# Expert weights in 4 MB transfers with 32 KB runs, and token rows dealt in fours

## The reference

```python
for e in range(N_EXPERTS):                       # 32
    gu = t @ w_gate_up[e] + b_gate_up[e]         # [1024] -> [2048]
    gate = jnp.minimum(gu[:, :D_EXPERT], SWIGLU_LIMIT)
    up = jnp.clip(gu[:, D_EXPERT:], -SWIGLU_LIMIT, SWIGLU_LIMIT)
    h = (up + 1.0) * (gate * jax.nn.sigmoid(SWIGLU_ALPHA * gate))
    out = out + comb[:, e:e + 1] * (h @ w_down[e] + b_down[e])
```

## Time and profile before

| what | value |
|---|---|
| time, median of 3 runs | 1209.77 us (1209.13 to 1209.91) |
| time of the profiled execution | 1210.05 us |
| its span | 1208.3 us |
| TensorE busy | 1169.4 us, 97% of the span |
| DMA | 446.82 MB, mean 370 GB/s |
| expert weights from 2 MB transfers in the ring | 125 of gate/up, 61 of down |

### The profile page before, as it was taken

How to read it: one execution, slowest core, us unless ns; L and a number is a source line. 1 busy time by engine, 2 the same in 40 slices (tenths; PEclk the granted TensorE clock), 3 DMA queues, 4 the chain that set the end, 5 groups by cost and what they waited for, 6 DMA issues and landing times.

```text
span 1208.3 us, 14638 instructions
## 1 busy us (share of the span) xinstructions
PE 1169.4 (97%) x5836; PEld 553.0 (46%) x5836; DVE 331.4 (27%) x864; ACT 213.7 (18%) x420; POOL 29.2 (2%) x64
## 2 busy tenths in 40 slices
PE   9999999999999999999989899999998999799997
PEld 7777777443443434343333333434434343334344
DVE  4844214250322222131312120313222212111223
ACT  2556302112010101101010112120101010101034
POOL 2001000000000000000000020000000000000000
PEclk9999999999999999999999999999999999999999
DMA  9935573679999999999999999999999999999961
GB/s 287 360 141 203 173 279 133 237 283 429 427 428 426 427 426 428 427 427 429 427 428 428 427 428 425 429 427 426 430 426 428 427 428 430 425 428 428 426 260 40
DMA packets 53287, 446.82 MB, mean 370 GB/s; under 512 B 8174, under 2 KB 11470, under 8 KB 28424
## 3 DMA queue, kind: packets, MB, share of 16 engines
q1 hardware_dynamic: 50512, 440.04, 87.8%
q0 software_dynamic: 2464, 5.71, 1.6%
q10 hardware_dynamic: 256, 0.30, 0.1%
HBM read 444.51 MB, written 1.88 MB: 369 GB/s over the span
## 4 chain that ended last, share of the span: by engine, by line
PE 78%; DMA 20%; ACT 1%; DVE 1%; issue 1%; SPq 0%; DVEq 0%
PE ps L1201 31%; PE ps L864 16%; DMA ring<-in_w_gate_up 14%; PE ps L1222 11%; PE ps L1236 4%; PE ps L1083 3%; DMA ring<-in_w_down 3%; DMA ring<-in_w_ple_gate 2%; PE ps L1016 2%; PE ps L1355 2%; PE ps L1178 2%; PE ps L1168 1%; PE ps L898 1%; PE ps L858 1%; PE ps L885 1%; PE ps L1076 1%
## 5 line engine op out<-in xcount | busy, mean ns | idle before, releaser
L1201 PE MATMUL ps<-ring,work 128*64 128x512 f32 x2000 | 443.6, 597 | 2.8 <-DMA ring<-in_w_gate_up 2.6
L1201 PEld LDWEIGHTS ps<-ring,work 128*64 128x64 f32 x2000 | 141.2, 138 | 273.6 <-issue 261.9
L1222 PE MATMUL ps<-ring,work 128*64 128x512 f32 x992 | 223.4, 595 | 19.4 <-DMA ring<-in_w_down 19.4
L864 PE MATMUL ps<-work,ring 128*128 128x288 f32 x736 | 180.6, 407 | 0.0
L864 PEld LDWEIGHTS ps<-work,ring 128*128 128x128 f32 x736 | 139.7, 190 | 39.6 <-issue 1.7
L1222 PEld LDWEIGHTS ps<-ring,work 128*64 128x64 f32 x992 | 70.6, 137 | 146.8 <-issue 127.6
L2122 DVE TENSOR_SCALAR work<-ps 128x512 f32<-128x512 f32 x32 | 22.1, 691 | 374.5 <-PE ps L1201 374.5
L2094 DVE TENSOR_TENSOR work<-ps,gain_pairs 128x256 f32<-128x256 f32 x60 | 25.5, 424 | 286.2 <-PE ps L1083 286.2
L1626 ACT ACTIVATE work<-work 128x512 f32<-128x512 f32 x32 | 20.2, 631 | 442.9 <-DVE work L2122 442.9
L1083 PE MATMUL ps<-work,x_tok 128*128 128x128 f32 x512 | 65.4, 285 | 0.0
L1083 PEld LDWEIGHTS ps<-work,x_tok 128*128 128x128 f32 x512 | 61.8, 197 | 3.9 <-issue 2.0
(11 more groups left out here) (286 smaller groups left out, 663.0 us busy)
## 6 DMA issues: line engine op xcount, KB each, us to landing
ring<-in_w_gate_up SPq DMA_DIRECT2D x125, 2048.0 KB, 29.5
ring<-in_w_down SPq DMA_DIRECT2D x61, 2048.0 KB, 29.6
ring<-in_w_in SPq DMA_DIRECT2D x7, 2048.0 KB, 19.0
work<-in_w_gate_up SPq DMA_DIRECT2D x3, 1536.0 KB, 12.9
ring<-in_w_proj_b SPq DMA_DIRECT2D x2, 2048.0 KB, 10.0
ring<-in_w_proj_a SPq DMA_DIRECT2D x2, 2048.0 KB, 10.1
ring<-in_w_out SPq DMA_DIRECT2D x2, 2048.0 KB, 9.4
ring<-in_w_ple_gate SPq DMA_DIRECT2D x4, 1024.0 KB, 28.6
```

The costliest lines, as they stand in the source:

```text
L864: mm = pe.matmul(out(b), lhs, rhs, start=(k == 0), stop=(k == len(pairs) - 1))
L1201: mm = pe.matmul(ps[half(g), b, :], xg[:, k, i % 2, :], blocks[2 * (k % 2) + at][:, 512 * g:512 * g + 512], start=False, stop=(k == KC - 1))
L1222: mm = pe.matmul(ps[half(g), b, :], hT_of[i % 2][:, 4 * j + k, :], blocks[k][:, 512 * g:512 * g + 512], start=False, stop=(4 * j + k == KC ...
```

## The change

- From piece 48 on (quad 2) two adjacent pieces come as one transfer of 4 MB, into two neighbouring places of the ring. A partition gets four rows of gate/up, or eight of down, in one run of 32 KB. SP waits before it for the second of the two pieces that held the places. The very last transfer stays apart: one of 2 MB and two of 1 MB.
- TensorE waits for the whole 4 MB before it uses the first of its pieces (`wait_expert_piece` waits on the first place's semaphore).
- The places of the ring are renumbered (`FRONT`, `MOE_SLOT`, `spare`), so that the two of each transfer are neighbours.
- Rows in fours ask for inputs in the same grouping. For pair 2 and later (`in_fours`) the pieces are read with that row order, also where they are still moved in 2 MB. ACT rewrites the two prompt tiles once in pair 1, `deal_inputs`, so that the gather reads contiguous columns, and eight small copies do it for the sample rows. GpSimd loads a second form of the gains, `gain_fours`.
- Down with eight rows in a partition asks that the two halves of the hidden values interleave. So every gate/up matmul, from pair 0 on, reads its moving row in runs of four elements with a step of eight (`dealt`), and its bias row too.

```diff
+        def two_pieces(q):
+            return ring[:, MOE_SLOT[q]:MOE_SLOT[q] + 2, :, :].rearrange("p s a b -> p (s a b)")
+        def dealt(row, g):
+            return row.rearrange("p (c g k) -> p c g k", g=2, k=RUN)[:, :, g, :]
+        def in_fours(m):
+            return not (isinstance(m, int) and m < 2)
...
             s, turn = place(Q, i, q)
-            eng.wait_ge(piece_landed[s], turn * 16 + 16)
+            first, turn = (s, turn) if isinstance(Q, int) and Q < OPENING else \
+                place(Q, *STREAM[STREAM.index((i, q)) // 2 * 2])
+            eng.wait_ge(piece_landed[first], turn * 16 + 16)
...
             def quad_pieces(quads, e0, last=False):
-                for at in range(QUAD_PIECES):
-                    ring_place_used(quads, at)
+                for at in range(0, QUAD_PIECES, 2):
                     i, q = STREAM[at]
-                    expert_piece((at - EXTRAS) % SLOTS, q, e0 + i, last and at == QUAD_PIECES - 1)
+                    r = (at - EXTRAS) % SLOTS
...
+                    ring_place_used(quads, at + 1)
+                    sp.dma_start(two_pieces(r), expert_rows(q, e0 + i)).then_inc(piece_landed[r], 16)
...
                             mm = pe.matmul(ps[half(g), b, :], xg[:, k, i % 2, :],
-                                           blocks[2 * (k % 2) + at][:, 512 * g:512 * g + 512],
+                                           dealt(blocks[2 * (k % 2) + at], g),
                                            start=False, stop=(k == KC - 1))
...
+            def deal_inputs():
+                for b in B_X:
+                    act.wait_ge(filled[b], inputs_gathered(b, 1, False))
+                for t in range(2):
+                    act.wait_ge(x1_copied, t + 1)
+                    nc.scalar.copy(x_tok[:, t, :].rearrange("p (j k c) -> p j k c", k=RUN, c=P),
+                                   x2[t].rearrange("p (j c k) -> p j k c", k=RUN, c=P)).then_inc(x1_dealt, 1)
+                act.wait_ge(comb_ready, 1)
...
                     if embeds and j == 1:
                         embedding_squares()
+                    if begins and j == 1:
+                        deal_inputs()
                     swish(m, 0)
```

More of the change, by code:

```diff
@@ L64 @@
 SLOTS = 8
[L66 to L70, removed]
+FRONT = [("in", 0, 7), ("in", 2, 0), ("in", 4, 3), ("in", 1, 4), ("in", 3, 5), ("in", 5, 6),
+         ("in", 6, 7), ("in", 7, 0), ("b", 0, 3), ("b", 1, 4), ("a", 0, 5), ("a", 1, 6),
+         ("out", 0, 7), ("out", 1, 0)]
+MOE_SLOT = [1, 2, 3, 4, 5, 6, 7, 0]
+RUN = 4
+DEALT_PARTS = 10
 CHUNK = {("gate", 0): (0, 3, 0), ("gate", 1): (0, 3, 1), ("hT", 1): (0, 3, 2),
@@ L266, in hybrid_layer @@
         iota_pass = sb("iota_pass", [P, PASSES])
-        spare = ring[:, 6:8, :, :].rearrange("p s a b -> p (s a b)")
+        spare = ring[:, 1:3, :, :].rearrange("p s a b -> p (s a b)")
         carved = [0]
@@ L673, in quad_pieces, with piece_half @@
+            def piece_half(q):
+                return slice(RUN * D * (q % 2), RUN * D * (q % 2) + RUN * D)
             def quad_pieces(quads, e0, last=False):
-                for at in range(QUAD_PIECES):
-                    ring_place_used(quads, at)
+                for at in range(0, QUAD_PIECES, 2):
                     i, q = STREAM[at]
-                    expert_piece((at - EXTRAS) % SLOTS, q, e0 + i, last and at == QUAD_PIECES - 1)
+                    r = (at - EXTRAS) % SLOTS
+                    if last and at == QUAD_PIECES - 2:
+                        ring_place_used(quads, at)
+                        sp.dma_start(whole_piece(r), expert_rows(q, e0 + i)[:, piece_half(q)]) \
+                            .then_inc(piece_landed[r], 16)
+                        ring_place_used(quads, at + 1)
+                        place_, src = whole_piece((r + 1) % SLOTS), expert_rows(q + 1, e0 + i)[:, piece_half(q + 1)]
+                        sp.dma_start(place_[:, 0:2 * D], src[:, 0:2 * D]).then_inc(last_half_landed, 16)
+                        sp.dma_start(place_[:, 2 * D:4 * D], src[:, 2 * D:4 * D]).then_inc(last_landed, 16)
+                        continue
+                    ring_place_used(quads, at + 1)
+                    sp.dma_start(two_pieces(r), expert_rows(q, e0 + i)).then_inc(piece_landed[r], 16)
@@ L684, in piece_rows @@
                 e = 4 * quads + i
-                if q < GU_PIECES:
+                if q < GU_PIECES and not in_fours(n // (QUAD_PIECES // 2)):
                     return w_gate_up[0, e, 2 * P * q:2 * P * q + 2 * P, :].rearrange("(p k) c -> p (k c)", k=2)
-                rows = 4 * P * (q - GU_PIECES)
-                return w_down[0, e, rows:rows + 4 * P, :].rearrange("(p k) c -> p (k c)", k=4)
+                return expert_rows(q, e)[:, piece_half(q)]
             def extra_rows(n, k, dst):
@@ L718, in opening_piece @@
                     return
-                later, at = divmod(n, QUAD_PIECES)
-                i, q = STREAM[at]
-                expert_piece(ring_turn(n) % SLOTS, q, 4 * later + i)
+                r = ring_turn(n) % SLOTS
+                sp.dma_start(whole_piece(r), piece_rows(n)).then_inc(piece_landed[r], 16)
             wait_filled(sp, ("gate", 3, 3))
@@ L1067, in _, with gather_samples @@
             turn_residual(1, 0)
-            x_blocks = [x_tok[:, t, :].rearrange("p (j c k) -> p j k c", c=P, k=2) for t in range(TT - 1)]
-            def gather_samples():
+            x_pairs = [x_tok[:, t, :].rearrange("p (j c k) -> p j k c", c=P, k=2) for t in range(TT - 1)]
+            x_fours = [x_tok[:, t, :].rearrange("p (j k c) -> p j k c", c=P, k=2) for t in range(TT - 1)]
+            def gather_samples(fours=False):
+                rows = sample_fours if fours else sample_rows
                 for k in range(2):
@@ L1075, in gather_samples, with gather_tile @@
                         own = own_quarter(q)
-                        pe.matmul(ps[:, b, k * P:k * P + P], sample_rows[own, k, :], sel[TT - 1][own, :],
+                        pe.matmul(ps[:, b, k * P:k * P + P], rows[own, k, :], sel[TT - 1][own, :],
                                   start=(k == 0), stop=False)
-            def gather_tile(q, t):
+            def gather_tile(q, t, fours=False):
                 last = t == TILES[-1]
+                x_blocks = x_fours if fours else x_pairs
                 for k in range(2):
@@ L1157, in gather @@
                     pe.wait_ge(emptied[b], inputs_gathered(b, m, late) - 1)
-                gather_samples()
+                if isinstance(m, int) and m == 2:
+                    pe.wait_ge(x1_dealt, DEALT_PARTS)
+                gather_samples(in_fours(m))
                 for q in range(QUARTERS):
                     for t in TILES[1:]:
-                        gather_tile(q, t)
+                        gather_tile(q, t, in_fours(m))
             def turn_hidden(m, s):
@@ L1177, in begin_sums @@
                 for g in range(2):
+                    row = bias_parts[0:BIAS_ROWS, at:at + D]
                     pe.matmul(ps[half(g), b, :], pick[0:BIAS_ROWS, :],
-                              bias_parts[0:BIAS_ROWS, at + 512 * g:at + 512 * g + 512],
+                              row[:, 512 * g:512 * g + 512] if kind == "out" else dealt(row, g),
                               start=True, stop=False)
@@ L1606, in copy_residual @@
                     nc.scalar.copy(x2[t], x1[t]).then_inc(x1_copied, 1)
+            def deal_inputs():
[6 more added lines that the diff above has]
+                act.wait_ge(comb_ready, 1)
+                src = flat_x[:, 2 * D:2 * D + QW].rearrange("p (c g k) -> p g k c", g=2, k=2)
+                for j in range(2):
+                    for g in range(2):
+                        for h in range(2):
+                            nc.scalar.copy(sample_fours[own_quarter(2 * j + g), :, 64 * h:64 * h + 64],
+                                           src[own_quarter(2 * j + h), g, :, :]).then_inc(x1_dealt, 1)
             def embedding_squares():
@@ L2092, in gathered @@
                     own = slice(2 * j, 2 * j + 2)
-                    gains = gain_pairs[:, own].unsqueeze(2).unsqueeze(3).to_broadcast([P, 2, 2, CAP])
+                    gains = (gain_fours if in_fours(m) else gain_pairs)[:, own].unsqueeze(2).unsqueeze(3) \
+                        .to_broadcast([P, 2, 2, CAP])
                     V.tensor_tensor(xg[:, own, :, :], ps[:, b, 0:2 * P].rearrange("p (c i s) -> p c i s", c=2, i=2), gains,
```

30 lines of the change are left out of this document (15 added, 15 removed).

## The result

The changed kernel takes 1224.64 us (median of 4 runs, 1224.0 to 1225.06) against 1209.45 us for the kernel before, a ratio of 1.0126 with a 95% interval of 1.0114 to 1.0138. It is slower by 15 us, 1.3%. The prediction was 1225.4. The profiled execution took 1225.06 us with a span of 1223.3, 15.0 us longer than the span before.

A forecast was written before the change was run, and what follows sets the result against it. Transfers set the pace, TensorE 4 to 5 us a pair faster. Queue standing 18.1 less 5.4 saved lands the last pieces at 1161.1; plus 23.38 gives 1184.5, 15.6 us later: 1225.7, less 0.28, 1225.4 us; range 1206.5 to 1230.

The forecast's parts named there:

- What long runs save: Weight stream, pieces 48 to 189: 71 transfers of 4 MB in 32 KB runs save 76 ns each, 5.4 us in all.
- The coarser step at the end: Pieces 188 and 189: TensorE starts when both have landed; 2.5 of 5.4 us left, or 2.9 us late without savings.
- The stores: GpSimd's 20 stores at pair 8: each small packet waits one weight run, so 29.7 us become 53.8, done at 772.6.
- The ring and its refilling: After pair 8's stall: full ring stops the weights' queue 14.1 us from 771, refilling adds 2.4 and 1.6, sum 18.1.
- Where a TensorE wait begins to cost: At pair 8: ACT's release after 759.6, with 107 freed by 771, costs about one us per us.
- the first rival: Stores at pair 8 not held up, or stretched at most 1.35 times: 2.5 us sooner, 1207.3 us; chance 0.19.
- the main sum: The likeliest case, stores stalling the weights' queue at pair 8: 18.1 us of standing queue, 1225.4 us; chance 0.66.
- Catching up: After pair 8: TensorE, some 17 us late, gains over 4 us a pair and waits again at pieces 188 and 189, 1161.1.
- What costs nothing: ACT's ten copies fit a 17.64 us idle gap in pair 1; the gains' load and matmuls reading in fours cost nothing.

The follow-up runs named there:

- the kernel with 11 stores: Changed kernel with the 16 stores of the sample states made into 7, so 11 stores in place of 20, same bytes: 1207.63 us, ratio 0.9985.
- the step alone: Kernel before with 4 MB transfers from piece 48 on, still in 16 KB runs, rows in pairs, no dealing: 1214.07 us, ratio 1.0036.
- the kernel before with 40 small transfers: Kernel before with 20 tiny loads added on GpSimd's queue ahead of the 20 stores, ACT waiting for all: 1219.86 us, ratio 1.0085.
- the kernels with 11 and 14: The kernel with 11 stores (1207.63 us), and the same with three tiny loads more that ACT waits for (1208.99 us).
- the faster version: Changed kernel with 11 stores, and pieces 188 and 189 sent as two 2 MB transfers with a semaphore each: 1205.42 us, ratio 0.9968.

## Why the prediction was right, step by step

The total came within 0.8 us of the forecast, and the path was the one described, but several terms were off by 1 to 3 us and cancelled, so that this closeness is partly luck.

- **What long runs save.** Right. TensorE's waits for the same down piece stood at 614.62 and 672.91 in the changed kernel, 58.29 us a pair, 9.715 a transfer, where 9.71 was worked out. In all 5.4 us were predicted. Summed over windows of 5 us from 440 to 1120, the kernel with 11 stores moved as much more than the kernel before as takes about 5.5 us at the full rate; the end of the wait for pieces 188 and 189 gained a little less, 1143.66 for 1148.01 in the step alone. The step alone ran at 428 GB/s, as before, so it is the run's length and not the transfer's size that saves.
- **The coarser step at the end.** The mechanism was right, its price too low. Predicted 2.9 us without long runs, measured 4.5; the missing 1.7 us is the lower clock after the wait of 2.5 us, which I had charged at pair 8 and at the loop's exit, but not here. In the changed kernel the first of the two pieces took 5.35 us instead of 3.65 too:

```profile
1159.04 5.35 PE L1255 MATMUL ps<-ring,work 128*64 128x512 f32 x16 [2.44 <-DMA ring<-in_w_down]
...
1183.89 6.68 PE L1388 MATMUL ps<-ring 128*128 128x512 f32 x15
```

  From 1159.04 to the tail's start at 1183.89 are 24.85 us, where 23.38 were worked out, and `w_ple_gate` no longer ends a wait.
- **The stores.** Right in the release but for 3.3 us, 769.34 for 772.6, and in its cause, shown by the kernel before with 40 small transfers and by the changed one with 11. The round was a little short of the 1.21 us taken: 335 packets on 16 engines in 24 us are 1.15 us for each. The weights' own small completions are packets too, and a store's packet that meets one of these waits almost nothing. That last is an argument, not shown.
- **The ring and its refilling.** Sum predicted 18.1 us of standing queue. The windows lack 1.6 us before 770, 10.0 to 780, 1.5 to 790, 2.5 to 795 and 2.2 to 820 (each its length less what GB/s over 430 make of it), 17.8: 13.1 where 14.1 were forecast for the first stop, 2.5 for 2.4 and 2.2 for 1.6. Two errors cancelled here: the weights ran out about 2.6 us earlier than 771, and 107 was used up 3.3 us earlier than 783.5. For the 1.6 us from the free place to the first data, which no row had shown, the trace has 1.2, from 780.23 to 781.4.
- **Where a TensorE wait begins to cost.** This part of the first rival was mis-sized. I put the point at 759.6 for ACT's release, with 107 used up by 771, and stretched stores by 1.35. With a release at 760.12 the kernel had already lost 7.7 us, at 754.56 about nothing. The runs put the point at about 764.8 for 107, where 771 was taken. Two steps failed. The time at which the ring is full was too late: the last weights moved at 769.2, and the mean of the engines ran out near 768.4. And the rival charged nothing for the issue and the gaps of the refilling, 5.6 us in the main sum, which would have put the point at 783.5 - 18.1 = 765.4. That beyond the point each us costs about one was right.
- **Catching up.** Right. TensorE was again waiting for pieces 188 and 189, at 1159.04 for 1161.1. Being 2.1 us sooner there and 1.5 us slower from there to the tail nearly cancel. Against the kernel with 11 stores the stream lacked about 17.2 us of bytes at 1120, but the pieces were awaited only 15.4 us longer; where the other 1.8 us went is open.
- **What costs nothing.** Right for the dealt reads; the ten copies were slower than the rows suggested (two took 3.95 us instead of 1.99, reading with a step) and still hidden.
- The Trainium skill's rule (DMA: Bandwidth & Descriptors, Queues, rings and completion order), that an engine goes round its queues a whole packet at a time, held here for packets of 32 KB: 335 to 336.

## What to carry to other kernels

Where a bulk stream fills the DMA engines, a small transfer on another queue is paid by the number of its packets, each at the price of one run of the bulk stream. Lengthening the runs makes every such transfer slower, so look first for those on whose completion anything waits, and merge them. Then work out how late the consumer may free its places before the stream stops, with the issue and the refilling counted in: up to there a wait is free, and well beyond it each us costs about one. A coarser transfer step is paid at the end of the stream, where a last pair can be sent in finer steps, and a longer wait for it can bring the lower clock as well.

## What the runs showed of the hardware

- A 32 KB run on this queue is one packet: the page counts 43095 packets for the same 446.82 MB that took 53287. Of the weights' queue alone, the step alone has 49376 packets and the changed kernel 40288, 9088 fewer, which is 71 transfers of 128 runs. The stream gained 0.8%, 58.74 to 58.29 us for 25 MB.
- A wait of TensorE of 2.4 to 2.6 us can be followed by matmuls at the lower level of the clock (16 in 5.35 or 5.13 us for 3.65), but not every time: in the kernel with 11 stores, after 2.50 us at 615.00 they took 5.13 (granted clock 0.70 over the next 5 us), after 2.50 us at 673.27 they took 3.65 (1.00). There three of six such waits were followed by slow matmuls, in the step alone, with waits of 2.54 to 2.58 us, all six. What decides is open. The times of the kernels with 11 and 14, which have this wait on the path of the end, spread over 2.7 and 4.0 us (1207.0 to 1209.7 and 1207.1 to 1211.1), where the kernel before spreads over 1.5 us; but the faster version, without the wait, spreads over 2.5, so the clock there is not the whole of it:

```profile
615.00 5.13 PE L1253 MATMUL ps<-ring,work 128*64 128x512 f32 x16 [2.50 <-DMA ring<-in_w_down]
...
673.27 3.65 PE L1253 MATMUL ps<-ring,work 128*64 128x512 f32 x16 [2.50 <-DMA ring<-in_w_down]
```

- ACT copied 128x1024 float32 in half the speed when the source was read with a step of four elements: 3.95 us for two copies against 1.99 for two contiguous ones.
